# One 2x2 block of weight chunks in seven block products instead of eight, in nine of eleven gate/up groups of two SwiGLU layers

## The reference

```python
D_MODEL, SEQ, FFN_DIM = 2048, 256, 5632
def swiglu(x, w_gate, w_up, w_down):
    return (jax.nn.silu(x @ w_gate) * (x @ w_up)) @ w_down
...
x = x + 0.5 * swiglu(rms_norm(x, ffn1_norm[l]), ffn1_w_gate[l], ffn1_w_up[l], ffn1_w_down[l])
...
x = x + jnp.concatenate([y_conv, y_attn], axis=-1) @ w_out[l]
x = x + 0.5 * swiglu(rms_norm(x, ffn2_norm[l]), ffn2_w_gate[l], ffn2_w_up[l], ffn2_w_down[l])
return rms_norm(x, final_norm)
```

## Time and profile before

| what | value |
|---|---|
| median of 3 runs | 1829.31 us (1829.03 to 1829.47) |
| the profiled execution, first to last instruction (its span) | 1827.1 us |
| PE busy | 1816.5 us, 99% |
| DVE busy | 1015.8 us, 56% |
| ACT busy | 829.3 us, 45% |
| matmuls with 512 moving columns | 7872 by the program's order |
| granted TensorE clock, mean | 0.999 |
| moved by DMA | 368.03 MB, mean 201 GB/s |

### The profile page before, as it was taken

The page is one execution under the profiler, slowest core; times in us unless marked ns, Lnnn a source line. Parts: engine busy times, 40 slices in busy tenths (PEclk is TensorE's granted clock), DMA queues, the critical chain, the costliest instruction groups (busy, mean ns, idle before and its releaser), DMA issues.

```text
span 1827.1 us, 22464 instructions
## 1 busy us (share of the span) xinstructions
PE 1816.5 (99%) x8105; PEld 1500.3 (82%) x8105; DVE 1015.8 (56%) x1237; ACT 829.3 (45%) x986; POOL 31.3 (2%) x36
## 2 busy tenths in 40 slices
PE   9999999999999999999999999999999999999998
PEld 7888888888888888888888888888888888888886
DVE  6555555555545555557657766555555555554554
ACT  6444444444444444545455455444444444443443
POOL 0000000000000000000000000000000000000000
PEclk9999999999999999999999999999999999999999
DMA  7666666666666656765665566666666666655554
GB/s 258 206 207 202 203 205 206 206 203 202 206 205 207 204 195 202 224 190 179 191 207 173 192 208 209 202 205 204 206 206 199 208 203 204 209 199 195 193 195 139
DMA packets 207563, 368.03 MB, mean 201 GB/s; under 512 B 19600, under 2 KB 37648, under 8 KB 207376
## 3 DMA queue, kind: packets, MB, share of 16 engines
q1 hardware_dynamic: 206784, 365.51, 63.2%
q0 software_dynamic: 144, 1.05, 0.2%
q10 hardware_dynamic: 576, 0.69, 0.1%
HBM read 347.25 MB, written 2.10 MB: 191 GB/s over the span
## 4 chain that ended last, share of the span: by engine, by line
PE 99%; DVE 0%; ACT 0%; DMA 0%; issue 0%; DVEq 0%; ACTq 0%
PE bank L382 33%; PE bank L384 33%; PE bank L383 33%; PE bank L508 0%; PE bank L525 0%; DMA x<-in_x_dram 0%; PE bank L420 0%; PE bank L439 0%; PE bank L516 0%; PE bank L533 0%; ACT x L629 0%; DVE w_lo L814 0%; ACT w_hi L596 0%; DVE xT_lo L834 0%; DVE xT_hi L1028 0%
## 5 line engine op out<-in xcount | busy, mean ns | idle before, releaser
L814 DVE TENSOR_TENSOR w_lo<-raw,w_hi 128x1024 fp32r<-128x1024 f32 x655 | 806.4, 1232 | 774.2 <-ACT w_hi L596 773.7
L596 ACT ACTIVATE w_hi<-raw 128x1024 fp32r<-128x1024 f32 x655 | 693.7, 1060 | 910.1 <-PE bank L384 905.3
L382 PE MATMUL bank<-w_hi,xT_hi 128*128 128x512 f32 x1788 | 699.3, 391 | 1.0 <-DVE w_lo L814 1.0
L384 PE MATMUL bank<-w_hi,xT_lo 128*128 128x512 f32 x1788 | 696.1, 389 | 0.0
L383 PE MATMUL bank<-w_lo,xT_hi 128*128 128x512 f32 x1788 | 695.8, 389 | 0.0
L382 PEld LDWEIGHTS bank<-w_hi,xT_hi 128*128 128x128 f32 x1788 | 335.6, 188 | 72.4 <-issue 3.8
L384 PEld LDWEIGHTS bank<-w_hi,xT_lo 128*128 128x128 f32 x1788 | 335.6, 188 | 70.1
L383 PEld LDWEIGHTS bank<-w_lo,xT_hi 128*128 128x128 f32 x1788 | 335.7, 188 | 68.8
L382 PE MATMUL bank<-w_hi,hT_hi 128*128 128x512 f32 x704 | 273.9, 389 | 0.0
L383 PE MATMUL bank<-w_lo,hT_hi 128*128 128x512 f32 x704 | 273.9, 389 | 0.0
L384 PE MATMUL bank<-w_hi,hT_lo 128*128 128x512 f32 x704 | 273.9, 389 | 0.0
(11 more groups left out here) (115 smaller groups left out, 418.2 us busy)
## 6 DMA issues: line engine op xcount, KB each, us to landing
raw<-in_ffn_w_up_dram SPq DMA_DIRECT2D x176, 512.0 KB, 3.7
raw<-in_ffn_w_down_dram SPq DMA_DIRECT2D x176, 512.0 KB, 3.6
raw<-in_ffn_w_gate_dram SPq DMA_DIRECT2D x175, 512.0 KB, 3.5
raw<-in_w_in_dram SPq DMA_DIRECT2D x96, 512.0 KB, 4.2
raw<-in_w_out_dram SPq DMA_DIRECT2D x32, 512.0 KB, 4.1
turn_in<-gate SPq DMA_DIRECT2D x448, 32.0 KB, 2.5
x<-in_x_dram SPq DMA_DIRECT2D x3, 512.0 KB, 8.7
out_dram<-x SPq DMA_DIRECT2D x6, 256.0 KB, 2.8
```

What stands on the lines that cost most here:

```text
L382: pe.matmul(acc, hi[:, kt, ts], w_hi[slot][:, kk], start=(k == 0 and kk == 0), stop=False)
L384: mm = pe.matmul(acc, lo[:, kt, ts], w_hi[slot][:, kk], start=False, stop=(k == chunks - 1 and kk == KC - 1))
L596: act.activation(w_hi[slot][:], raw[slot][:], ACT.Copy).then_inc(hi_ready, 1)
L814: dve.tensor_tensor(w_lo[slot][:], raw[slot][:], w_hi[slot][:].bitcast(F32), ALU.subtract)\
```

## The change

In groups 1 to 9 of both FFNs (`MIXED`) the last two chunks of gate and the last two of up, which are a 2x2 block (two row halves by gate and up), meet the two halves of the tokens: eight products of a half of the tokens with a chunk, 6 matmuls each. They are replaced by seven products of sums (Winograd's form of Strassen's scheme), P1 to P7, 6 matmuls each. The other 12 chunks stay units (G0 to G5 of gate, U0 to U5 of up).

- PE: a group is now 19 *forms* (12 units, 7 products) in the order G0 G1 G2 P1 G3 P5 P2 G4 P6 P4 G5 P7 P3 U0 U1 U2 U3 U4 U5. The ring of four `w_hi`/`w_lo` buffers counts forms. PE also waits for copies of partial sums (`snapped`).
- Weights: the four chunks of the block are loaded into buffers of their own (`blocks`, over the last part of `hT`), during the U units of the group before. DVE makes four sums of chunks per group (`outer_sums`, `first_sum`, `second_sum`, `third_sum`). ACT and DVE split all seven factors, so 19 `high` and 19 `low` per group for 16.
- Activations: sums of halves are made once per FFN in group 0 (`token_sum`, 11 DVE operations on 256 columns, then a split into `s_hi`, `s_lo`).
- Results: ACT copies banks four times per group (`snapshot`), DVE adds to gate (`gate_sum`), ACT takes Silu from SBUF, DVE adds to up and then multiplies 1024 columns (`up_sums`).
- Transposing of the hidden group: `turn_quads` now stands at the end of the group itself, straight behind `up_sums`. The 16 small DMAs stand in one row on SP, behind the load of G4 of the next group. ACT's `split_hidden` stands behind its third `high` of the next group, DVE's behind its seventh `low`.
- The loops over groups are written out, on every engine. The load of `gfin` waits for the end of FFN 2's gate/up stage, because `s_hi` and `s_lo` share its storage.

The diff, cut to its core:

```diff
+NORM = CD - 2
+KA, KB = CD - 2, CD - 1
+P1, P2, P3, P4, P5, P6, P7 = range(1, 8)
+G0, G1, G2, AT_P1, G3, AT_P5, AT_P2, G4, AT_P6, AT_P4, G5, AT_P7, AT_P3, U0, U1, U2, U3, U4, U5 = range(19)
+AT = {P1: AT_P1, P2: AT_P2, P3: AT_P3, P4: AT_P4, P5: AT_P5, P6: AT_P6, P7: AT_P7}
+PLAIN = (G0, G1, G2, G3, G4, G5, U0, U1, U2, U3, U4, U5)
+FORMS = 2 * NORM + 7
+MIXED = range(1, GROUPS - 1)
...
+                blocks += [part(f"block_{half}{n}", [P, KC, W]) for n in range(2)]
...
+        b11, b12, b21, b22 = (b[:] for b in blocks)
+        s_f = diff[:].rearrange("p k n -> p (k n)").rearrange("p (s k n) -> p s k n", s=4, k=KC)
+        source = {P1: b11, P5: b12, P6: b11, P2: b21, P4: b21, P7: diff[:], P3: b22}
...
+            def load(f, w, pair, col):
+                m = RAW_OF[f]
+                if m >= RING:
+                    sp.wait_ge(lo_ready, FORM_OF_RAW[m - RING] + 1)
                 src = w[0].rearrange("(k p) n -> p k n", p=P)[:, KC * pair:KC * pair + KC, bass.ds(col, W)]
-                sp.dma_start(raw[slot][:], src).then_inc(raw_loaded[slot], 16)
+                sp.dma_start(raw[m % RING][:], src).then_inc(raw_loaded[m % RING], 16)
+            def load_block(ch, c, to, name, freed_by, w, pair):
+                if c > MIXED[0]:
+                    sp.wait_ge(lo_ready, ch + group_form(c - 1) + AT[freed_by] + 1)
+                src = w[0].rearrange("(k p) n -> p k n", p=P)[:, KC * pair:KC * pair + KC, c * W:(c + 1) * W]
+                sp.dma_start(to, src).then_inc(block_loaded[name], 16)
...
+            def next_blocks(base, wg, wu, c, k):
+                if c not in MIXED:
+                    return
+                if k == 1:
+                    load_block(base, c, b11, "b11", P6, wg, KA)
+                if k == 2:
+                    load_block(base, c, b12, "b12", P5, wu, KA)
+                if k == 3:
+                    load_block(base, c, b22, "b22", P3, wu, KB)
+                if k == 4:
+                    load_block(base, c, b21, "b21", P4, wg, KB)
...
-                        load(base + 2 * CD * c + CD * u + k, k % RING, w, k, c * W)
-                        if u == 1 and k < QUADS and not first:
-                            move_hidden(f, c, k)
+                        load(base + group_form(c) + CD * u + k, w, k, c * W)
+                        if u == 1 and first:
+                            if k == 1 and f == 1:
+                                sp.wait_ge(chunk_used, CH_FFN2)
+                            next_blocks(base, wg, wu, c + 1, k)
+                        if u == 0 and k == 4 and not first:
+                            for q in range(QUADS):
+                                move_hidden(f, c, q)
...
+            def mixed_group(f, base, wg, wu, c):
+                b = base + group_form(c)
+                for k, at in enumerate((G0, G1, G2, G3, G4, G5)):
+                    load(b + at, wg, k, c * W)
+                    if k == 4:
+                        for q in range(QUADS):
+                            move_hidden(f, c, q)
+                for k, at in enumerate((U0, U1, U2, U3, U4, U5)):
+                    load(b + at, wu, k, c * W)
+                    next_blocks(base, wg, wu, c + 1, k)
...
+            def product(f, to, hi, lo, opens=False, seen=False, on_sums=False):
+                pe.wait_ge(lo_ready, f + 1)
+                slot = f % RING
+                acc = bank[to][:]
+                for kk in range(KC):
+                    pe.matmul(acc, hi[:, kk], w_hi[slot][:, kk], start=(opens and kk == 0), stop=False,
+                              skip_group_check=on_sums)
+                    pe.matmul(acc, hi[:, kk], w_lo[slot][:, kk], start=False, stop=False, skip_group_check=on_sums)
+                    mm = pe.matmul(acc, lo[:, kk], w_hi[slot][:, kk], start=False, stop=(seen and kk == KC - 1),
+                                   skip_group_check=on_sums)
+                mm.then_inc(chunk_used, 1)
+            def mixed_group(ch, pr, c, quad):
+                b = ch + group_form(c)
+                half = KC * KA, KC * KB
+                a11 = [x[:, half[0]:half[0] + KC, 0:P] for x in (xT_hi, xT_lo)]
+                a12 = [x[:, half[1]:half[1] + KC, 0:P] for x in (xT_hi, xT_lo)]
+                a22 = [x[:, half[1]:half[1] + KC, P:2 * P] for x in (xT_hi, xT_lo)]
+                s1, s2, s3, s4 = ((s_hi[:, n], s_lo[:, n]) for n in range(4))
+                banks_free(pr + c, 0)
+                plain(b + G0, 0, 0, opens=True)
+                plain(b + G1, 0, 1)
+                plain(b + G2, 0, 2)
+                banks_free(pr + c, 1)
+                product(b + AT[P1], 3, *a11, opens=True, seen=True)
+                plain(b + G3, 0, 3)
+                if c == MIXED[0]:
+                    pe.wait_ge(token_lo, 1 + quad // len(MIXED))
+                product(b + AT[P5], 2, *s1, opens=True, seen=True)
+                product(b + AT[P2], 0, *a12)
+                plain(b + G4, 0, 4)
+                pe.wait_ge(snapped, 4 * quad + 1)
+                product(b + AT[P6], 3, *s2, seen=True, on_sums=True)
+                product(b + AT[P4], 1, *a22)
+                plain(b + G5, 0, 5, ends=True)
+                pe.wait_ge(snapped, 4 * quad + 3)
+                product(b + AT[P7], 3, *s3, seen=True, on_sums=True)
+                product(b + AT[P3], 2, *s4, on_sums=True)
+                plain(b + U0, 1, 0, wait_for=4 * quad + 4, on_sums=True)
+                for k, at in enumerate((U1, U2, U3, U4)):
+                    plain(b + at, 1, k + 1, on_sums=True)
+                plain(b + U5, 1, 5, ends=True, on_sums=True)
...
+            def snapshot(to, of, f, scale=1.0):
+                act.wait_ge(chunk_used, f + 1)
+                act.activation(to, bank[of][:], ACT.Copy, scale=scale).then_inc(snapped, 1)
+            def gate_summed(pair, t):
+                act.wait_ge(drained[0], pair * TT + t + 1)
+                act.activation(gate[:, t], gate[:, t], ACT.Silu, scale=rstd[:, t:t + 1]).then_inc(gated, 1)
...
+            def mixed_group(ch, pr, hid, c):
+                b = ch + group_form(c)
+                high(b + G0 + RING)
+                high(b + G1 + RING)
+                high(b + G2 + RING)
+                split_hidden(hid, c - 1)
+                high(b + AT[P1] + RING)
+                snapshot(gate[:, 0], 3, b + AT[P1])
+                high(b + G3 + RING)
+                high(b + AT[P5] + RING)
+                high(b + AT[P2] + RING)
+                high(b + G4 + RING)
+                act.wait_ge(hid_lo, hid + c)
+                snapshot(turn_in[:, 1], 2, b + AT[P5], scale=rstd[:, 1:2])
+                high(b + AT[P6] + RING)
+                high(b + AT[P4] + RING)
+                snapshot(turn_in[:, 0], 3, b + AT[P6], scale=rstd[:, 0:1])
+                high(b + G5 + RING)
+                gate_summed(pr + c, 0)
+                snapshot(gate[:, 1], 3, b + AT[P7])
+                high(b + AT[P7] + RING)
+                high(b + AT[P3] + RING)
+                gate_summed(pr + c, 1)
+                for at in (U0, U1, U2, U3, U4, U5):
+                    high(b + at + RING)
...
+            def outer_sums(quad, ch, c):
+                if c == MIXED[0]:
+                    dve.wait_ge(token_lo, 1 + quad // len(MIXED))
+                else:
+                    dve.wait_ge(lo_ready, ch + group_form(c - 1) + AT[P7] + 1)
+                dve.wait_ge(block_loaded["b12"], 16 * (quad + 1))
+                dve.wait_ge(block_loaded["b22"], 16 * (quad + 1))
+                dve.tensor_tensor(diff[:], b22, b12, ALU.subtract).then_inc(blocks_summed, 1)
+            def first_sum(quad):
+                dve.wait_ge(block_loaded["b11"], 16 * (quad + 1))
+                dve.tensor_tensor(b12, b12, b11, ALU.subtract).then_inc(blocks_summed, 1)
+            def second_sum(quad, b):
+                dve.wait_ge(lo_ready, b + AT[P1] + 1)
+                dve.wait_ge(blocks_summed, 4 * quad + 2)
+                dve.tensor_tensor(b11, b22, b12, ALU.subtract).then_inc(blocks_summed, 1)
+            def third_sum(quad, b):
+                dve.wait_ge(lo_ready, b + AT[P2] + 1)
+                dve.wait_ge(blocks_summed, 4 * quad + 3)
+                dve.tensor_tensor(b21, b21, b11, ALU.subtract).then_inc(blocks_summed, 1)
...
+            def gate_sum(pair, f, t, snaps):
+                dve.wait_ge(snapped, snaps)
+                unit_done(f + 1, pair, 0, t)
+                dve.tensor_tensor(gate[:, t], bank[t][:], gate[:, t], ALU.add).then_inc(drained[0], 1)
+            def up_sums(pair, f, quad, c, hid):
+                dve.wait_ge(snapped, 4 * quad + 4)
+                for t in range(TT):
+                    unit_done(f + 1, pair, 1, t)
+                    dve.scalar_tensor_tensor(out=turn_in[:, t], in0=bank[2 + t][:], scalar=rstd[:, t:t + 1],
+                                             in1=turn_in[:, t], op0=ALU.mult, op1=ALU.add).then_inc(drained[1], 1)
+                dve.wait_ge(gated, TT * (quad + 1))
```

(63 more changed lines are left out.)

194 lines of the change are left out of this document (147 added, 47 removed).

## The result

The change takes 1925.05 us (median of 4 runs, 1922.3 to 1927.36) where the kernel before takes 1829.36 (1829.03 to 1829.47): 1.0523 times as long, 95% interval 1.051 to 1.0535. Slower, as forecast, but 56 us above the forecast of 1869 and 30 above the upper end of the range. The profiled execution spans 1920.0 us, 92.9 more than before.

What follows compares the result with a forecast made beforehand. PE bounds the kernel, busy 1816.5 of 1827.1 us. Per mixed group 3.5 + 0.2 - 1.36 = +2.35 us, +1.1 in each FFN's first: +39.8 us in all, giving 1869 us by the median; range 1848 to 1895.

Steps and rivals of the forecast that it cites:

- Taken out: PE, 18 mixed groups: six matmuls fewer in each, 108 x 0.227 = 24.5 us saved.
- Added on DVE and ACT: Extra splits, sums and copies on DVE and ACT: high load but no bound, costed at nothing.
- Steps 1 to 5, the wait at G4: Mixed groups: DVE's transposing, 16 issues on SP, landing, then ACT's and DVE's splits make PE wait 3.5 us at G4.
- the moves are early enough: Rival: SP issues the row faster or DVE turns earlier, G4's w_lo is ready, all 24.5 us gained: 1805; chance 0.06.
- The break-even: SP's row: with PE's wait at 1.36 us moves must land by 12.7, needing under 0.47 us each.
- Step 6, 0.2 us at P7: Mixed groups: ACT's copy of P6's bank ends about when PE asks before P7; wait 0.2 us (0 to 0.5).
- The first mixed group: First mixed group of each FFN: no multiplication in the group before, moves start 1.2 us earlier, net +1.1 us.
- Group 10 is plain, its `split_hidden` stands behind seven high (about 19): no wait: Plain group 10 of each FFN: split_hidden comes at about 19 us, so no wait.
- Step 7: SP's loads behind the moves: G5's, issued at 13.3, lands at 17.0, before ACT needs it (19.4); hidden.
- The wait puts PE's clock down: Rival: PE's 3.5 us waits halve its clock, 1.6 us lost each, 29 us over 18: 1898; chance 0.18.
- More comes late than I follow: Rival: delayed loads in the U units, 0.5 to 1 us per group: 1878 to 1887; chance 0.1.

Runs made afterwards that it cites:

- both: two_queues and split_later together, on top of g10_moves_back: 1805.67 us, ratio 0.987 to the kernel before.
- two_queues: g10_moves_back with 8 of the 16 small DMAs per mixed group issued by POOL instead of SP: 1806.53 us, ratio 0.9875 to the kernel before.
- split_later: g10_moves_back with split_hidden behind six high on ACT, ahead of the seventh low on DVE, and the row of moves behind G5's load: 1807.68 us.
- g10_moves_back: The change with plain group 10's 16 small DMAs put back between the loads of its first four up chunks: 1904.15 us.
- clock_kept: g10_moves_back with 12 extra matmuls, into a bank nobody reads, before G4 in groups 1 to 9: 1877.76 us.

## Why the prediction was right and wrong

*Taken out* held: 24.5 us are there for the taking, as `both` shows, all but 0.9. *Added on DVE and ACT*, at nothing, held too, by the same run.

*Steps 1 to 5, the wait at G4*, held: 3.5 forecast, 3.69 measured. SP's issuing time is the cause, not the data, which `two_queues` and `split_later` show from two sides. That the number is so close is in part luck. Take the group whose first matmul starts at 244.40: the row starts 3.9 us later (3.65 forecast), lasts 10.02 (9.7) and lands 1.3 after its end (1.6), and PE waits 3.40. So small errors cancelled there, and the mean lies above 3.5 only by the six waits behind a long issue, which the forecast did not have. ACT's idle time was 6.0 in the mean (108.3 / 18) for 5.5. The rival "the moves are early enough" fell: a row of sixteen goes at the rate of a row of four. The Trainium skill gives the sequencer's dispatch as about 50 ns ("DMA: Bandwidth & Descriptors", anatomy of one DMA). No issue here was near that: SP was held 0.63 us by each and POOL 0.49; what share of these is dispatch the rows do not tell. The break-even was put at under 0.47 us per move on one queue; `two_queues` passes it, as SP is through its eight in 4.96 us.

*Step 6, 0.2 us at P7*, was nothing. ACT and DVE had caught up by then.

*The first mixed group*, taken as 1.2 us better, was not. There DVE's pair starts only at 55.95, behind a sum that group 0 has at 54.82, and the moves only at 58.72; the waits are 3.29 and 3.22, not 2.3. About 2 us in all.

*"Group 10 is plain, its `split_hidden` stands behind seven high (about 19): no wait"* is the first step that failed. The forecast asked whether `hT_hi` would come in time and not what else stood behind the row. *Step 7* did ask it, with the right numbers, but for the mixed groups alone. The same numbers give the wait: the load issued at 13.3 lands at 17.0, `high` and `low` put it at 19.3, and PE comes to G5 after five units, at 13.6. That is 5.7 us of wait; 6.70 and 7.05 were measured, and 20.9 us in the total with the clock behind them. `g10_moves_back` shows it.

*"The wait puts PE's clock down" at 0.18*, with the likeliest case at nothing, is the second step that failed, and the larger: 37.1 us, and without them the measured time would be 1888, inside the range. The row at the program's end had PE idle for 3.2 us before the clock fell, and the forecast held that "not each wait need be long enough or be caught". It fell in 17 of 20. What the tail could not show is that the fall also comes once PE has begun again: at 1398.36, in the second FFN, five matmuls stood 0.23 to 0.34 us apart before the steps went to 0.43. So a wait that ends before the fall isn't safe from it. The size, "1.6 us lost per wait", was close: 1.42 by `clock_kept`, and 1.86 with the restart, over 20 waits and not over 18. The Trainium skill's rule on idle gaps between bursts ("TensorE: Matmul & The Clock Gate"), which I set beside this rival, is what the rows show here in 17 of 20 cases, at 1.42 us per gap of `clock_kept`.

With those two steps right the sum would have been 1829.3 - 24.5 + 60.5 + 3.6 + 11.4 + 20 x 1.6 = 1912, 13 us below the measured time. The rest is 6.0 at G4, 2.4 in group 10 and 5.1 of clock and restart, less the 3.6 at P7 that did not come, and 2.8 by which the changed kernel's median lies above its profiled execution (1922.3).

*More comes late than I follow*, in the U units: no such wait.

## What to carry to other kernels

Price a row of small DMAs as their number times the issuing time on that queue, read from the trace, and then list what stands behind the row on the queue in every form of the loop body, the untouched one first: the load behind it is as late as the data in it. A consumer of such a row goes behind as much work as possible that doesn't need it, or the row goes on two queues; either one, once the plain group's moves were back in their place, turned 4% slower into 1.2% faster here. And price an isolated wait on a busy TensorE above its own length: behind waits of 3.2 to 7 us the clock fell in 17 of 20 cases, behind waits of 9 us in all 20, and each wait cost 1.4 to 2 us more in PE's busy time. Waits of up to 1.64 us (`clock_kept`) cost 0.3.

## What was not expected of the hardware

- In 11 of 17 falls the granted clock goes down only after the work has begun again, one to five matmuls later; it stays at half for 5 to 8 matmuls of 427 ns, in three cases for 12 or 13. One and the same wait, at G4 of the first mixed group, ended with a fall in `g10_moves_back` (3.27 us) and without one in the change (3.29 us).
- Behind a short wait the second matmul starts 0.34 us after the first (steps are 0.227); with the last matmul before the wait, which nothing overlaps, that is 0.3 us of busy time per wait.
- The same small DMA costs POOL's queue 0.49 us (8 in 3.92) and SP's 0.63 (16 in 10.02). In seven of the change's 20 rows a single issue took 1.08 to 1.71 us; what held it up is not known.

Not tried: seven products in groups 0 and 10 as well, and fewer but larger moves than sixteen.
